# The mean of each residual norm is made by VectorE instead of GpSimd in a fused three-layer decoder kernel

## The chip, the cores and the metric

The kernel runs on one core of a Trainium2 chip. The metric is the device time of one execution in microseconds (us), smaller is better. All tensors are fp32; the matmuls run on operands split into a high and a low part (type fp32r).

## The reference, cut to what matters

Two blocks run one after the other on a residual `x` of 256 rows by 1024 columns. The first has two layers of mixer, cross-attention and SwiGLU, the second has one layer of three gated branches and a convolutional GLU. What matters here is the norm that opens each part:

```python
def rms_norm(x, gain):
    x32 = x.astype(jnp.float32)
    y = x32 * lax.rsqrt(jnp.mean(x32 * x32, axis=-1, keepdims=True) + RMS_EPS)
    return (y * gain.astype(jnp.float32)).astype(x.dtype)
...
    for layer in range(DEPTH):
        hn = rms_norm(x, g[0])                # mixer (norms 0 and 3 of the kernel)
...
        x = x + rms_norm(y, g[1])
        y = memory_cross_attention(rms_norm(x, g[2]), ...)   # norms 1 and 4
        x = x + rms_norm(y, g[3])
        y = swiglu_ffn(rms_norm(x, g[4]), ...)               # norms 2 and 5
        x = x + rms_norm(y, g[5])
...
    h = _rmsnorm(x, norm_mix_g[l])            # norm 6
    x = x + (merged @ w_out[l].astype(jnp.float32)).astype(x.dtype)
    h2 = _rmsnorm(x, norm_ffn_g[l])           # norm 7
```

## The kernel before, in words

The five engines run five programs that are written out by hand, in a fixed order on each, and meet at named semaphores. The residual lies in SBUF as two tiles of 128 rows by 1024 columns (`xr[:, t, :]`, t = 0 and 1), and `xn` holds the normed rows.

**Weights.** SyncE streams them in chunks of 1 MB, each cut into two pieces of 128x1024. ScalarE rounds a piece to its high part (`whi`, L1124) and VectorE subtracts to get the low part (`wlo`, L1663). TensorE multiplies with both. Both engines work up to four pieces ahead of TensorE (`past(name)` does all pieces up to four behind the chunk of that name). So between any two steps of the program VectorE and ScalarE have weight pieces to do, and their place in the order is fixed.

**A norm of the residual** (eight of them, `no` = 0 to 7) is a chain over four engines, for each of the two tiles:

1. ScalarE squares a tile with the row sums as accumulator (`squares`, L1142; norm 7 squares each half of a tile, L1624), semaphore `n_sq` (`half_sq`).
2. GpSimd makes the mean plus epsilon (L2291; L2427 in norm 7), waits on its own semaphore `pool_step`, and takes the power -0.5 (L2292; L2428), semaphore `n_r`. Both are on one column of 128 rows.
3. VectorE multiplies the tile with that column (`normed`, L1683), semaphore `n_x`.
4. TensorE turns the tile in eight 128x128 transposes (L472; L1093 in norm 7), ScalarE takes the high part with the gain (L1156; L1634) and VectorE the low part (`rest`, L1693; L2257), eight of each, semaphores `n_hi` and `n_lo`. The next matmuls (L388 to L390 of `fm`, L403 and L405 of `wide`, L418 and L420 of `wide_tile` in norm 7) wait for these.

Between the end of the block before and the matmuls that need the normed rows TensorE has filler work: products of the memory rows (`keys`, `values`, the `mk` and `mv` chunks), put before, between and behind the transposes. Norm 0, at the start, has none; norm 7 has the last pieces of the `mo` product. In norms 1 to 6 VectorE has two weight pieces (`past(...)`) between the last residual addition (`post_add`, L1715) and `normed`, and two more behind it, and often a copy out of PSUM (L1726), before the first `rest`.

Of the kernel before, what the change touches and what calls it, by code (L numbers as in the profile page):

```python
# [5 lines left out]
ALU = mybir.AluOpType  # L6
ACT = mybir.ActivationFunctionType
# [6 lines left out]
EPS = 1e-6  # L14
BIG = -1.0e30
D = 1024
# [9 lines left out]
h_A01m h_cp h_d h_e h_f h_m1 h_m2 h_n h_o h_q h_r h_sq h_z half_sq heads_T heads_a heads_d heads_n hg_act  # L26
hn_r hn_sq hn_ss ho_r ho_sq ho_ss lg_zero lo_first m2_act m2_dve mT_T mT_hi mT_lo m_T m_hi m_lo m_r m_sq m_x
mem0_in0 mem0_in1 mem1_in0 mem1_in1 mg mg0 ml_act ml_cols ml_dec ml_dve ml_hs ml_log ml_num ml_og ml_p ml_qk
ml_z mlv_act mlv_dve mo_add mt n_T n_hi n_lo n_r n_sq n_x out pa_m pa_r pa_sq pool_step resid row_in0 row_in1
row_in2 row_in3 row_in4 row_in5 sb_a sb_c sb_hi sb_k sb_ln sb_lo sb_q sb_t sb_v sb_w sb_z sbv_act sbv_dve  # L30
tm_first w_first w_hi w_lo w_raw0 w_raw1 w_raw2 w_used x_in0 x_in1 xe xm xo xo_hi xp xq xs xt xv xw ya_hi
ya_lo yb_hi yb_lo z_T z_hi z_lo
"""

SHARED = {
# [48 lines left out]
def build_program(nc, I, out):  # L84
    ctx = ExitStack()
    with ctx:
        def sb(name, shape, dt=F32):
            return ctx.enter_context(nc.sbuf_tensor(name, shape, dt))
# [6 lines left out]
        xr = sb("xr", [128, NT, D])  # L95
        xn = sb("xn", [128, NT, D])
# [13 lines left out]
        mhalf = sb("mhalf", [128, 8])  # L110
# [18 lines left out]
        def stats(n):  # L129
            return [(stat(n), stat(n), stat(n)) for _ in range(NT)]  # L130
# [140 lines left out]
        S = {}  # L271
# [14 lines left out]
        n_st = [stats(1) for _ in range(8)]  # L286
        half_sq = [(stat(1), stat(1)) for _ in range(NT)]
# [21 lines left out]
        xq = [reg(512 * i, 512).rearrange("p (k t) -> p k t", k=2) for i in range(3)]  # L309
# [800 lines left out]
        def scalar_program(act):  # L1110
# [25 lines left out]
            def squares(no):  # L1136
                for t in range(NT):
                    if no == 0:
                        act.wait_ge(S[f"x_in{t}"], 16)
                    else:  # L1140
                        act.wait_ge(S["resid"], 2 * no - 1 + t)
                    act.activation(xn[:, t, :], xr[:, t, :], ACT.Square, accum_out=n_st[no][t][0]).then_inc(S["n_sq"], 1)  # L1142

            def mem_squares(i):
                for t in range(NT):
# [160 lines left out]
            for t in range(NT):  # L1306
                act.wait_ge(S["ml_hs"], t + 1)
                for h in range(4):
                    if t or h:
                        act.wait_ge(S["h_sq"], 4 * t + h)  # L1310
                    act.activation(sq[:, 0:256], heads(xn[:, t, :], 4)[:, h, :], ACT.Square,
                                   accum_out=h_st[t][0][:, h:h + 1]).then_inc(S["h_sq"], 1)
# [8 lines left out]
            for k in range(8):  # L1321
                b, half = half_bank(k, (0, 1, 2, 3))
                act.wait_ge(S["z_T"], k + (1 if half else 3))
                if half:
                    act.wait_ge(S["z_lo"], k - 1)
                act.activation(XTh[:, k, :], ps[:, b, 256 * half:256 * half + 256], ACT.Copy,
                               scale=g[:, k:k + 1]).then_inc(S["z_hi"], 1)
# [322 lines left out]
        def vector_program(dve):  # L1650
# [28 lines left out]

            def normed(no, tiles=range(NT)):  # L1680
                for t in tiles:
                    dve.wait_ge(S["n_r"], 2 * no + t + 1)
                    dve.tensor_scalar(xn[:, t, :], xr[:, t, :], n_st[no][t][2], None, ALU.mult).then_inc(S["n_x"], 1)  # L1683

# [594 lines left out]
        def gpsimd_program(pool):  # L2279
            own = [0]  # L2280

            def step(i):
                own[0] += 1
                i.then_inc(S["pool_step"], 1)
                return own[0]

            def rstd(stat3, n, cnt, sem, need, done):

                ss, m, r = stat3
                pool.wait_ge(*at(sem, need))  # L2290
                pool.wait_ge(S["pool_step"], step(pool.tensor_scalar(m, ss, 1.0 / cnt, EPS, ALU.mult, ALU.add)))  # L2291
                pool.tensor_tensor(r, m, mhalf[:, 0:n], ALU.pow).then_inc(S[done], 1)  # L2292

            def norm(no):
                for t in range(NT):
                    rstd(n_st[no][t], 1, D, "n_sq", 2 * no + t + 1, "n_r")

            def mem_norm(i):
                for t in range(NT):
# [122 lines left out]
                        pool.wait_ge(S["mg"], 2 * n + t - 1)  # L2422
                    pool.tensor_tensor(dst, dst, bt[:, 512 * t:512 * t + 512], ALU.add).then_inc(S["mg"], 1)
            for t in range(NT):
                ss, m, r = n_st[7][t]
                pool.wait_ge(S["half_sq"], 2 * t + 2)
                pool.wait_ge(S["pool_step"], step(pool.tensor_scalar(m, half_sq[t][0], half_sq[t][1], EPS, ALU.add, ALU.add)))  # L2427
                pool.tensor_tensor(r, m, mhalf[:, 0:1], ALU.pow).then_inc(S["n_r"], 1)  # L2428


        def sync_program(sp):
# [67 lines left out]
```

## Time and profile before

| | |
|---|---|
| median of 3 runs | 1312.08 us (1310.54 to 1313.65) |
| the profiled execution: time | 1310.67 us |
| its span | 1308.9 us |
| TensorE busy | 1289.3 us, 99% of the span |
| VectorE busy | 882.5 us, 67% |
| ScalarE busy | 688.8 us, 53% |
| GpSimd busy | 111.0 us, 8% |
| chain that ended last, by engine | TensorE 90%, VectorE 5%, ScalarE 3%, GpSimd 1%, issue 1%, DMA 1% |

The span is the time from the first to the last instruction of the profiled execution; 1.8 us of its time lie outside it. TensorE sets the pace nearly everywhere; the shares of the other engines in the chain are the short places at which TensorE waited.

### The profile page before, as it was taken

The page shows a single profiled execution, that of the slowest core. Times are in us where ns is not written, and L with a number is a line of the kernel's source. Part 1 is how long each engine was busy: PE and PEld are TensorE (multiplying, and loading weights), DVE is VectorE, ACT ScalarE, POOL GpSimd, SP SyncE. Part 2 cuts the span into 40 slices and gives each one's busy share as a digit, 9 for nine tenths or more (in the row PEclk, how much of TensorE's full clock was granted, in tenths as well). Part 3 has the DMA queues.
Part 4 walks back from the last instruction along what each step waited for, and adds up shares of the span by engine and source line. Part 5 has one row for each costly group of instructions (what it writes and reads, how often), then busy time and mean ns, then how long its engine had stood idle before and what let it go on. Part 6 is the DMA issues. An engine that isn't in the chain of part 4 may idle for free.

```text
span 1308.9 us, 17685 instructions
## 1 busy us (share of the span) xinstructions
PE 1289.3 (99%) x7313; PEld 1109.8 (85%) x7313; DVE 882.5 (67%) x1035; ACT 688.8 (53%) x960; POOL 111.0 (8%) x176
## 2 busy tenths in 40 slices
PE   7999999999999999999999999999999999999999
PEld 6889897988888888788888888898877888888887
DVE  4566664776666676876576666767885566887775
ACT  4655554644444656564554444565555654654553
POOL 7200100100000100030100000101330003000000
PEclk9999999999999999999999999999999999999999
DMA  8753653555555543354356555563544435455552
GB/s 260 246 169 134 198 172 104 196 193 187 187 188 188 189 161 124 135 178 144 129 192 194 190 188 184 178 194 98 161 149 143 159 131 191 135 188 192 193 194 97
DMA packets 156113, 223.64 MB, mean 171 GB/s; under 512 B 6103, under 2 KB 107635, under 8 KB 156032
## 3 DMA queue, kind: packets, MB, share of 16 engines
q1 hardware_dynamic: 154240, 218.18, 50.7%
q0 software_dynamic: 1664, 4.27, 1.1%
q8 instruction: 58, 0.95, 0.3%
q14 instruction: 23, 0.19, 0.0%
q10 hardware_dynamic: 128, 0.05, 0.0%
HBM read 221.44 MB, written 1.05 MB: 170 GB/s over the span
## 4 chain that ended last, share of the span: by engine, by line
PE 90%; DVE 5%; ACT 3%; POOL 1%; issue 1%; DMA 1%; SPq 0%; ACTq 0%
PE ps L403 18%; PE ps L405 9%; PE ps L450 9%; PE ps L451 9%; PE ps L452 9%; PE ps L388 5%; PE ps L390 5%; PE ps L389 5%; PE ps L585 4%; PE ps L587 4%; PE ps L586 4%; DVE wlo L1663 2%; PE ps L897 1%; PE ps L472 1%; ACT whi L1124 1%; PE ps L520 1%
## 5 line engine op out<-in xcount | busy, mean ns | idle before, releaser
L1124 ACT ACTIVATE whi<-raw 128x1024 fp32r<-128x1024 f32 x412 | 425.9, 1052 | 347.1 <-PE ps L403 163.7
L1663 DVE TENSOR_TENSOR wlo<-raw,whi 128x1024 fp32r<-128x1024 f32 x411 | 492.9, 1229 | 169.8 <-ACT whi L1124 166.9
L403 PE MATMUL ps<-RR,whi 128*128 128x512 f32 x1040 | 359.1, 396 | 0.0
L405 PE MATMUL ps<-RR,wlo 128*128 128x256 f32 x1040 | 268.9, 279 | 0.1
L450 PE MATMUL ps<-whi,RR 128*128 128x512 f32 x592 | 238.3, 402 | 3.1 <-DVE ar L1726 1.6
L452 PE MATMUL ps<-whi,RR 128*128 128x512 f32 x592 | 231.0, 390 | 0.0
L451 PE MATMUL ps<-wlo,RR 128*128 128x512 f32 x592 | 231.0, 390 | 0.0
L403 PEld LDWEIGHTS ps<-RR,whi 128*128 128x128 f32 x1040 | 187.6, 188 | 35.9
L405 PEld LDWEIGHTS ps<-RR,wlo 128*128 128x128 f32 x1040 | 196.0, 188 | 12.1 <-DVE RR L1693 0.4
L388 PE MATMUL ps<-RR,whi 128*128 128x256 f32 x512 | 147.3, 288 | 2.9 <-DVE RR L1693 1.4
L390 PE MATMUL ps<-RR,wlo 128*128 128x256 f32 x512 | 144.8, 283 | 0.0
L389 PE MATMUL ps<-RR,whi 128*128 128x256 f32 x512 | 144.8, 283 | 0.0
L450 PEld LDWEIGHTS ps<-whi,RR 128*128 128x128 f32 x592 | 111.2, 188 | 30.3 <-issue 3.6
L452 PEld LDWEIGHTS ps<-whi,RR 128*128 128x128 f32 x592 | 111.1, 188 | 24.2
L451 PEld LDWEIGHTS ps<-wlo,RR 128*128 128x128 f32 x592 | 111.3, 188 | 21.2
L388 PEld LDWEIGHTS ps<-RR,whi 128*128 128x128 f32 x512 | 98.1, 192 | 6.3 <-DVE RR L1693 2.9
L585 PE MATMUL ps<-whi,RR 128*128 128x512 f32 x256 | 99.7, 389 | 0.0
L587 PE MATMUL ps<-whi,RR 128*128 128x512 f32 x256 | 99.6, 389 | 0.0
L586 PE MATMUL ps<-wlo,RR 128*128 128x512 f32 x256 | 99.6, 389 | 0.0
L389 PEld LDWEIGHTS ps<-RR,whi 128*128 128x128 f32 x512 | 98.1, 192 | 0.2
L390 PEld LDWEIGHTS ps<-RR,wlo 128*128 128x128 f32 x512 | 98.1, 192 | 0.0
L1764 DVE TENSOR_REDUCE ar<-ps 128x512 f32<-128x1024 f32 x33 | 40.4, 1225 | 74.0 <-PE ps L403 73.2
(337 smaller groups left out, 1279.2 us busy)
## 6 DMA issues: line engine op xcount, KB each, us to landing
raw<-in_ffn_w_gate_up SPq DMA_DIRECT2D x44, 1024.0 KB, 5.1
raw<-in_ffn_w_down SPq DMA_DIRECT2D x33, 1024.0 KB, 5.0
raw<-in_w_in SPq DMA_DIRECT2D x28, 1024.0 KB, 5.1
raw<-in_ffn_w_up SPq DMA_DIRECT2D x22, 1024.0 KB, 5.1
raw<-in_xa_w_kv SPq DMA_DIRECT2D x16, 1024.0 KB, 5.2
raw<-in_sb_w_qkv SPq DMA_DIRECT2D x12, 1024.0 KB, 5.1
raw<-in_ml_w_in SPq DMA_DIRECT2D x11, 1024.0 KB, 7.8
raw<-in_xa_w_q SPq DMA_DIRECT2D x8, 1024.0 KB, 5.3
```

The costliest lines, as they stand in the source:

```text
L388: pe.matmul(o, p.hi[:, k, :], X.h[:, k, :], start=k == 0, stop=False)
L389: pe.matmul(o, p.hi[:, k, :], X.l[:, k, :], start=False, stop=False)
L390: m = pe.matmul(o, p.lo[:, k, :], X.h[:, k, :], start=False, stop=k == 7)
L403: m = pe.matmul(two(ps[:, bank, :]), p.hi[:, k, :], XT2[:, k, :, :], start=k == 0, stop=k == 7)
L405: pe.matmul(ps[:, bank, 0:256], p.lo[:, k, :], X.h[:, k, :], start=False, stop=False)
L450: pe.matmul(o, X.h[:, g, r], p.hi[:, k, :], start=g == 0, stop=False)
L451: pe.matmul(o, X.h[:, g, r], p.lo[:, k, :], start=False, stop=False)
L452: m = pe.matmul(o, X.l[:, g, r], p.hi[:, k, :], start=False, stop=g == K - 1)
L585: pe.matmul(o, h[:, i, r], p.hi[:, 0, c], start=j == 0 and i == 0, stop=False)
L586: pe.matmul(o, h[:, i, r], p.lo[:, 0, c], start=False, stop=False)
L1124: act.activation(p.hi, p.raw, ACT.Copy).then_inc(S["w_hi"], 1)
L1663: dve.tensor_tensor(p.lo, p.raw, p.hi.bitcast(F32), ALU.subtract).then_inc(S["w_lo"], 2 if p.n == 2 else 1)
```

## The change

ScalarE squares `x / 32` instead of `x` (a scale of the same activation, 1024 ** -0.5), so that its row sums are already the means. VectorE adds epsilon in `normed`, ahead of each tile's multiplication: for norms 0 to 6 it waits for ScalarE's sum, for norm 7 it adds the two halves' sums and epsilon. GpSimd waits for that (new semaphore `n_m`) and takes the power alone. The other uses of GpSimd's `rstd` (`post_norm`, `mem_norm`, the head norms) stay as they are.

```diff
-                    act.activation(xn[:, t, :], xr[:, t, :], ACT.Square, accum_out=n_st[no][t][0]).then_inc(S["n_sq"], 1)
+                    act.activation(xn[:, t, :], xr[:, t, :], ACT.Square, scale=D ** -0.5,
+                                   accum_out=n_st[no][t][0]).then_inc(S["n_sq"], 1)
...
             def normed(no, tiles=range(NT)):
                 for t in tiles:
+                    ss, m, r = n_st[no][t]
+                    if no < 7:
+                        dve.wait_ge(S["n_sq"], 2 * no + t + 1)
+                        dve.tensor_scalar(m, ss, EPS, None, ALU.add).then_inc(S["n_m"], 1)
+                    else:
+                        dve.wait_ge(S["half_sq"], 2 * t + 2)
+                        dve.tensor_scalar(m, half_sq[t][0], half_sq[t][1], EPS, ALU.add, ALU.add).then_inc(S["n_m"], 1)
                     dve.wait_ge(S["n_r"], 2 * no + t + 1)
                     dve.tensor_scalar(xn[:, t, :], xr[:, t, :], n_st[no][t][2], None, ALU.mult).then_inc(S["n_x"], 1)
...
+            def root(no, t):
+
+                ss, m, r = n_st[no][t]
+                pool.wait_ge(S["n_m"], 2 * no + t + 1)
+                pool.tensor_tensor(r, m, mhalf[:, 0:1], ALU.pow).then_inc(S["n_r"], 1)
+
             def norm(no):
                 for t in range(NT):
-                    rstd(n_st[no][t], 1, D, "n_sq", 2 * no + t + 1, "n_r")
+                    root(no, t)
...
             for t in range(NT):
-                ss, m, r = n_st[7][t]
-                pool.wait_ge(S["half_sq"], 2 * t + 2)
-                pool.wait_ge(S["pool_step"], step(pool.tensor_scalar(m, half_sq[t][0], half_sq[t][1], EPS, ALU.add, ALU.add)))
-                pool.tensor_tensor(r, m, mhalf[:, 0:1], ALU.pow).then_inc(S["n_r"], 1)
+                root(7, t)
```

First, VectorE's order at norm 4, from the last residual addition of the block before (L1715, L1723 in the changed file) to the first low parts of the turned rows. Before:

```order
L1715 SCALAR_TENSOR_TENSOR xr<-xn,st,xr 128x1024 [waits pa_r,pa_m]
L1663 TENSOR_TENSOR wlo<-raw,whi 128x1024 [waits w_hi] x2
L1683 TENSOR_SCALAR xn<-xr,st 128x1024 [waits n_r] x2
L1678 COPY gcol<-ps 128x88 [waits gains_T]
L1663 TENSOR_TENSOR wlo<-raw,whi 128x1024 [waits w_hi] x2
L1693 SCALAR_TENSOR_TENSOR RR<-ps,gcol,RR 128x256 [waits n_hi] x8
```

And with the change (every line number is a few higher, so L1691 is the multiplication that was L1683):

```order
L1723 SCALAR_TENSOR_TENSOR xr<-xn,st,xr 128x1024 [waits pa_r,pa_m]
L1664 TENSOR_TENSOR wlo<-raw,whi 128x1024 [waits w_hi] x2
L1686 TENSOR_SCALAR st<-st 128x1 [waits n_sq]
L1691 TENSOR_SCALAR xn<-xr,st 128x1024 [waits n_r]
L1686 TENSOR_SCALAR st<-st 128x1 [waits n_sq]
L1691 TENSOR_SCALAR xn<-xr,st 128x1024 [waits n_r]
L1679 COPY gcol<-ps 128x88 [waits gains_T]
L1664 TENSOR_TENSOR wlo<-raw,whi 128x1024 [waits w_hi] x2
L1701 SCALAR_TENSOR_TENSOR RR<-ps,gcol,RR 128x256 [waits n_hi] x8
```

The additions stand in VectorE's queue behind the two weight pieces, and the second tile's addition behind the first tile's multiplication. Norms 1, 2, 3, 5 and 6 have the same five rows around `xn<-xr,st`.

Second, the same engine at norm 7, from the additions of the two half products into the residual (L2250; L2258 in the changed file) to the second tile's multiplication. Before:

```order
L2250 TENSOR_TENSOR xr<-xr,ps 128x512 [waits tm_first] x2
L1683 TENSOR_SCALAR xn<-xr,st 128x1024 [waits n_r]
L2250 TENSOR_TENSOR xr<-xr,ps 128x512 [waits w_used]
L1663 TENSOR_TENSOR wlo<-raw,whi 128x1024 [waits w_hi] x2
L2257 SCALAR_TENSOR_TENSOR RR<-ps,gcol,RR 128x128 [waits n_hi] x4
```

And with the change:

```order
L2258 TENSOR_TENSOR xr<-xr,ps 128x512 [waits tm_first] x2
L1689 TENSOR_SCALAR st<-st 128x1 [waits half_sq]
L1691 TENSOR_SCALAR xn<-xr,st 128x1024 [waits n_r]
L2258 TENSOR_TENSOR xr<-xr,ps 128x512 [waits w_used]
L1664 TENSOR_TENSOR wlo<-raw,whi 128x1024 [waits w_hi] x2
```

Here nothing stands between the half products' additions and the new instruction.

Third, GpSimd's order around norm 4, between its DMA of the second memory and the norm of that memory (`m_sq`). Before:

```order
L2390 DMA ar<-in_mem 128x1024
L2291 TENSOR_SCALAR st<-st 128x1 [waits n_sq]
L2292 TENSOR_TENSOR st<-st,mhalf 128x1 [waits pool_step]
L2291 TENSOR_SCALAR st<-st 128x1 [waits n_sq]
L2292 TENSOR_TENSOR st<-st,mhalf 128x1 [waits pool_step]
L2291 TENSOR_SCALAR st<-st 128x1 [waits m_sq]
L2292 TENSOR_TENSOR st<-st,mhalf 128x1 [waits pool_step]
```

And with the change (L2306 is the power in `root`):

```order
L2404 DMA ar<-in_mem 128x1024
L2306 TENSOR_TENSOR st<-st,mhalf 128x1 [waits n_m] x2
L2299 TENSOR_SCALAR st<-st 128x1 [waits m_sq]
L2300 TENSOR_TENSOR st<-st,mhalf 128x1 [waits pool_step]
L2299 TENSOR_SCALAR st<-st 128x1 [waits m_sq]
```

GpSimd now waits for VectorE where it waited for ScalarE, and has one instruction per tile and no wait on itself.

## Rows read from the trace of the kernel before

**Rows 1.** The page: busy time (share of the span) and instructions

```profile
PE 1289.3 (99%) x7313; PEld 1109.8 (85%) x7313; DVE 882.5 (67%) x1035; ACT 688.8 (53%) x960; POOL 111.0 (8%) x176
PEclk9999999999999999999999999999999999999999
```

**Rows 2.** Who TensorE waited for: us in total, times, longest

```profile
PE ps L472 <- DVE xn L1683: 2.7, 1, 2.7
...
PE ps L388 <- DVE RR L1693: 1.4, 3, 0.5
```

**Rows 3.** The chain that ended last, around norm 6: start, us, what

```profile
844.89 1.41 POOL st L2292
846.39 0.76 POOL st L2291
847.23 0.56 POOL st L2292
847.81 0.75 DVE xn L1683
...
852.97 0.39 PE ps L388
```

**Rows 4.** Timeline at norm 6: start, us, instruction, [idle before <-releaser]

```profile
843.54 2.35 DVE L1663 TENSOR_TENSOR wlo<-raw,whi 128x1024 fp32r<-128x1024 f32 x2
...
846.34 0.75 DVE L1683 TENSOR_SCALAR xn<-xr,st 128x1024 f32<-128x1024 f32 x1 [0.45 <-POOL st L2292]
```

**Rows 5.** One line of VectorE: a TENSOR_SCALAR on one column

```profile
L2138 DVE TENSOR_SCALAR st<-gcol x1: 145/145/145, 962.1 to 962.1; 128x1 f32<-128x1 f32 x1
```

**Rows 6.** Timeline: a small result handed from VectorE to GpSimd

```profile
945.64 0.69 DVE L2112 TENSOR_REDUCE st<-ar 128x4 f32<-128x512 f32 x1 [0.84 <-ACT ar L1521]
946.42 0.20 POOL L2291 TENSOR_SCALAR st<-st 128x4 f32<-128x4 f32 x1 [7.08 <-DVE st L2112]
```

**Rows 7.** Chain around norm 5

```profile
658.81 0.39 PE ps L405
```

**Rows 8.** Timeline at norm 3

```profile
435.46 2.35 DVE L1663 TENSOR_TENSOR wlo<-raw,whi 128x1024 fp32r<-128x1024 f32 x2
...
440.00 0.76 DVE L1683 TENSOR_SCALAR xn<-xr,st 128x1024 f32<-128x1024 f32 x1 [0.72 <-POOL st L2292]
...
445.16 0.39 PE L388 MATMUL ps<-RR,whi 128*128 128x256 f32 x1 [0.50 <-DVE RR L1693]
```

**Rows 9.** Timeline at norm 4

```profile
571.14 2.36 DVE L1663 TENSOR_TENSOR wlo<-raw,whi 128x1024 fp32r<-128x1024 f32 x2
571.36 1.43 POOL L2292 TENSOR_TENSOR st<-st,mhalf 128x1 f32<-128x1 f32 x1
574.61 0.75 DVE L1683 TENSOR_SCALAR xn<-xr,st 128x1024 f32<-128x1024 f32 x1 [0.44 <-POOL st L2292]
...
578.78 1.66 DVE L1693 SCALAR_TENSOR_TENSOR RR<-ps,gcol,RR 128x256 fp32r<-128x256 f32 x4 [0.21 <-ACT RR L1156]
579.83 0.28 PE L388 MATMUL ps<-RR,whi 128*128 128x256 f32 x1
```

**Rows 10.** Timeline at norm 7, first tile

```profile
1111.52 0.19 ACT L1624 ACTIVATION_READ_ACCUMULATOR xn<-xr 128x1 f32 x1
1112.20 0.57 POOL L2428 TENSOR_TENSOR st<-st,mhalf 128x1 f32<-128x1 f32 x1
1112.81 0.75 DVE L1683 TENSOR_SCALAR xn<-xr,st 128x1024 f32<-128x1024 f32 x1 [1.86 <-POOL st L2428]
1116.84 0.36 PE L418 MATMUL ps<-RR,whi 128*128 128x256 f32 x1 [0.27 <-DVE RR L2257]
```

**Rows 11.** Chain in the first 20 us

```profile
2.16 7.47 DMA raw<-in_ml_w_in
```

**Rows 12.** Timeline behind norms 1 and 2, VectorE

```profile
157.92 4.98 DVE L1663 TENSOR_TENSOR wlo<-raw,whi 128x1024 fp32r<-128x1024 f32 x4
...
247.99 1.23 DVE L1663 TENSOR_TENSOR wlo<-raw,whi 128x1024 fp32r<-128x1024 f32 x1 [0.46 <-ACT whi L1124]
```

More of the change, by code:

```diff
@@ L28 @@
 mem0_in0 mem0_in1 mem1_in0 mem1_in1 mg mg0 ml_act ml_cols ml_dec ml_dve ml_hs ml_log ml_num ml_og ml_p ml_qk
[L29 to L32, printed above, removed]
+ml_z mlv_act mlv_dve mo_add mt n_T n_hi n_lo n_m n_r n_sq n_x out pa_m pa_r pa_sq pool_step resid row_in0
+row_in1 row_in2 row_in3 row_in4 row_in5 sb_a sb_c sb_hi sb_k sb_ln sb_lo sb_q sb_t sb_v sb_w sb_z sbv_act
+sbv_dve tm_first w_first w_hi w_lo w_raw0 w_raw1 w_raw2 w_used x_in0 x_in1 xe xm xo xo_hi xp xq xs xt xv xw
+ya_hi ya_lo yb_hi yb_lo z_T z_hi z_lo
 """
```

## Prediction

> **What bounds the kernel now.** I read the page first: TensorE is busy 99% of the span at the full granted clock, VectorE 67%, GpSimd 8% [rows 1]. A change to GpSimd and VectorE can therefore only move time where TensorE waits for the result. The waits of TensorE come next: in all, it waited 2.7 us once for `xn` (norm 0, at the start) and 1.4 us in three places for the low parts of the turned rows [rows 2]. The chain that ended last then says which of these lead back through a norm's GpSimd steps. At norm 6 it does: power, mean, power on GpSimd, VectorE's multiplication, and 5 us later the matmul that had waited [rows 3]. The chain runs the same way to TensorE's wait at 658.81 behind norm 5 [rows 7], to that at 445.16 behind norm 3 [rows 8], and through norm 7's first tile [rows 10]. At norm 0 it goes through the DMA of the first weights instead [rows 11]; at norms 1, 2 and 4 it stays on TensorE.
>
> So the change is priced norm by norm, and the number wanted for each is when VectorE's *second* multiplication ends, since the weight pieces, the copy and the low parts behind it run in one unbroken row.
>
> **The new path, once.** Prices: the addition on one column 0.145 us, from VectorE's own one-column TENSOR_SCALAR [rows 5]; VectorE to GpSimd 0.09 us (945.64 + 0.69 = 946.33 to 946.42) [rows 6]; the power undisturbed 0.56 us [rows 3] to 0.57 us [rows 10], of which I take 0.55 in norms 0 to 6, since the chain's pieces reach to the next one's start; GpSimd to VectorE 0.04 us (1112.77 to 1112.81) [rows 10]. VectorE starts an instruction for which nothing is awaited about 0.08 us before the profile's end of the one before it. From the end of what VectorE did before, the path "add, hand over, power, hand back" is then -0.08 + 0.145 + 0.09 + 0.55 + 0.04 = 0.745 us.
>
> **Norm 6, and norm 5 like it.** Before, GpSimd works while VectorE does its two weight pieces (843.54 to 845.89). The mean is done and the power issued at 844.89, and it ended at 846.30, only 0.41 us after the pieces, though alone it takes 0.55 [rows 3, 4]. VectorE multiplied at 846.34. With the change the addition stands behind the pieces: multiplication at 845.89 + 0.745 = 846.63, +0.29. Second tile: before, GpSimd's mean ran under the multiplication (846.34 to 847.09) and ended at 847.15, 0.06 us behind it; power at 847.23, multiplication at 847.81, that is 0.72 us after the first one's end [rows 3]. Now it is 0.745, so +0.30 in all after rounding.
> The stretched GpSimd rows (0.76 instead of 0.19, ending with a VectorE instruction) are the wait for the shared port. The Trainium skill, "SBUF — State Buffer", section "Who interferes with whom", says that the loser of that port fully blocks for the other's whole instruction, and its section on the wrong bandwidth intuition gives "DVE-end + ~115 ns" before it goes on. By that, the power would have ended at 845.89 + 0.115 + 0.55 = 846.56, the change would cost only 0.07 + 0.03 us at norms 5 and 6, and the sum below would be about 0.4 us smaller; the row has 846.30, so part of the power had been done behind the lock, and I take the row.
> At norm 6 TensorE's matmul at 852.97 follows VectorE directly [rows 3]: **+0.30**. Norm 5 has the same order on all engines, and TensorE waited at 658.81 in its chain [rows 7]: **+0.30**.
>
> **Norm 3.** ScalarE's sum came late, so that little of GpSimd's work lay under the weight pieces, which end at 437.81; the second multiplication began at 440.00 [rows 8]. With the change: first multiplication at 438.555, second 0.75 + 0.745 later at 440.05. TensorE at 445.16 follows: **+0.05**.
>
> **Norm 4.** Here ScalarE's sums came early and the first power had ended (571.36 + 1.43 = 572.79) before the weight pieces did (573.50): the first multiplication waited for nothing, and the second began at 574.61 [rows 9]. With the change: 573.50 + 0.745 = 574.245, ends 574.995; the second at 574.995 + 0.745 = 575.74, that is 1.13 late. What is late next: TensorE's transposes of the second tile, by less than that, and then the low parts, which all move by 1.13. One of them takes (1.66 + 3 x 0.08) / 4 = 0.475 us; the third ends at 578.78 + 0.475 + 1.13 = 580.385, and TensorE, which began to use it at 579.83 without a wait [rows 9], begins at 580.45. **+0.62**, in which the transposes' delay is contained. Behind that VectorE idles between weight pieces as it does behind norm 2 [rows 12], and makes its delay good.
>
> **Norm 7.** ScalarE's sum is there at 1111.71, VectorE is idle. Before: multiplication at 1112.81 [rows 10]. Now: 0.04 (nearest row, GpSimd to VectorE; ScalarE to GpSimd would be 0.11) + 0.16 (my estimate for the addition with a column as its second operand, a little over the 0.145) + 0.09 + 0.57 + 0.04 = 1112.61. TensorE's wait at 1116.84 is in this chain. **-0.20**. The second tile gains as much, but TensorE reaches its transposes after `xn` is there, so it adds nothing.
>
> **Norms 0, 1, 2.** At norm 0 the multiplications come some 0.15 us earlier; the chain there is a DMA until 9.63 us and ScalarE's rounding behind it [rows 11], which hide it (uncovered it would be worth -0.15). At norms 1 and 2 VectorE is 0.30 late as at norm 6. Behind norm 1 the four weight pieces take 4.98 us where two take 2.35, so they hold 0.3 us of waits for ScalarE that absorb it; behind norm 2 the low parts end 0.46 us before VectorE's next weight piece is ready [rows 12], and TensorE waits in neither stretch. **0** each; without this cover +0.6 together.
> ScalarE's scale adds no instruction. GpSimd loses sixteen small instructions: it is idle anyway.
>
> **Sum.** 0.30 + 0.30 + 0.05 + 0.62 - 0.20 = +1.07 us. The profiled execution would go from 1310.67 to 1311.7 us. That one lies 1.4 us under the median of the runs, 1312.08, so against the median I give **1313.1 us**, +0.08%. Changes under 0.2% (2.6 us; the three runs before spread over 3.1 us) can't be told from none.
>
> **Bounds.** The addition could cost less on the path only if VectorE began it earlier, which its order excludes; if the first power before the change had hidden nothing at norms 5 and 6 (it then could not end before 845.89 + 0.55 = 846.44, 0.14 later than it did) and norm 4's delay meets 0.3 us of slack that I don't see, the sum is 1.07 - 0.28 - 0.3 = +0.5. If the additions take 0.25 us and nothing covers norms 1 and 2, it is 1.07 + 0.6 + 8 x 0.1 = +2.5.
>
> **Rivals.**
> *The chain shortens (faster).* Counting only GpSimd's steps, the chain at norm 6 holds a mean of 0.76 us [rows 3]; if each tile of norms 3, 5 and 6 lost that and got 0.15 instead, 6 x 0.6 = 3.6 us would go, 1308.5. Against it: most of each 0.76 is VectorE's own work, under which the mean ran; taking it away does not bring VectorE's next result sooner. It decides if GpSimd's power starts while VectorE still works, which the order forbids. 3 in 100.
> *Nothing arrives (same).* TensorE's waits at norms 4 to 6 are met by slack the trace doesn't show: 1312.1. 15 in 100.
> *The granted clock falls (slower).* Norm 4 adds pauses of 0.6 us in all to a stretch in which TensorE ran without one. Were the clock to be granted at 1.2 GHz instead of 2.4 behind it, each us of TensorE's work costs another; it decides when more than 1.5 us of work fall in it, and 4 us of it give 1317. Against it: the page has 9 or more tenths in all forty slices, though TensorE waited 2.7 us at once at the start [rows 1, 2]. 4 in 100. The Trainium skill, "TensorE: Matmul & The Clock Gate", section "What's actually happening", says that idleness brings the throttle back; the pauses here are far shorter than the one at the start, behind which the rows show none.
> *The late VectorE work piles up (slower, by the same path).* All eight norms uncovered and the dearer addition: the +2.5 above, 1314.6, just under what can be told. 8 in 100.
> The forecast has the remaining 70.
>
> **Chances.** Faster by over 0.2%: 0.03, the first rival. Slower by over 0.2%: the clock, a part of the last rival, and the median's own scatter on top of +1.07, together 0.09. Same: 0.88. The range reaches from the case in which nothing arrives (1312.1) less 0.9 us of scatter to the +2.5 (1314.6) and 0.4 us of it: 1311.2 to 1315.0.
>
> **What would show it.** Around norm 4 (from 570 us) the second `xn` multiplication starts about 2.2 us after the second weight piece's end instead of 1.1, and the first L388 after the transposes shows a wait of 0.3 to 0.6 us for the low parts. At norms 5 and 6 each multiplication starts 0.75 us after the end of VectorE's work before it. The power is 0.55 us at all sixteen places, never 1.43. At norm 7 the gap from ScalarE's sum to the multiplication is 0.9 instead of 1.1 us. The prediction is wrong if a power is still stretched, if the addition takes over 0.25 us, or if TensorE's row of busy time shows new waits outside the norms.

## The result, and the profile after

| | before | changed |
|---|---|---|
| median | 1310.74 us (22 runs, 1310.08 to 1313.65) | 1313.18 us (22 runs, 1311.63 to 1315.70) |
| ratio | | 1.0017, 95% interval 1.0011 to 1.0023 |
| the profiled execution: time, span | 1310.67, 1308.9 us | 1312.99, 1311.2 us |

The medians are 2.44 us apart, 0.19%, just within what I took as no difference. The interval excludes 1.0: the change costs a little. (The ratios here are the recorded ones; they are not quotients of the two medians, which would be 1.0019 in this table.) The times of either kernel lie in groups. The lowest seven runs of the changed one are 1311.63 to 1311.71 us; the lowest fourteen of the kernel before are 1310.08 to 1310.8. These groups are about 1.1 us apart, the rest of the 2.44 lies in how many runs fall in higher groups. Both parts are followed below.

The page of the changed kernel, busy time and the chain by engine:

```profile
PE 1291.6 (99%) x7313; PEld 1111.2 (85%) x7313; DVE 883.8 (67%) x1051; ACT 688.8 (53%) x960; POOL 96.3 (7%) x160
PE 90%; DVE 6%; ACT 2%; issue 1%; DMA 1%; POOL 0%; SPq 0%; ACTq 0%
```

Sixteen instructions and 14.7 us left GpSimd, sixteen and 1.3 us came to VectorE, and of the chain GpSimd's 1% is gone, VectorE has 6% instead of 5 and ScalarE 2% instead of 3. Beside [rows 1] this reads like a relief; it is none. The timeline at norm 6, VectorE and then GpSimd, shows why (start, us, instruction, idle before and who ended it):

```profile
845.82 2.35 DVE L1664 TENSOR_TENSOR wlo<-raw,whi 128x1024 fp32r<-128x1024 f32 x2
848.09 0.14 DVE L1686 TENSOR_SCALAR st<-st 128x1 f32<-128x1 f32 x1
848.90 0.75 DVE L1691 TENSOR_SCALAR xn<-xr,st 128x1024 f32<-128x1024 f32 x1 [0.66 <-POOL st L2306]
849.57 0.14 DVE L1686 TENSOR_SCALAR st<-st 128x1 f32<-128x1 f32 x1
850.38 0.75 DVE L1691 TENSOR_SCALAR xn<-xr,st 128x1024 f32<-128x1024 f32 x1 [0.66 <-POOL st L2306]
...
848.32 0.55 POOL L2306 TENSOR_TENSOR st<-st,mhalf 128x1 f32<-128x1 f32 x1 [4.08 <-DVE st L1686]
849.79 0.55 POOL L2306 TENSOR_TENSOR st<-st,mhalf 128x1 f32<-128x1 f32 x1 [0.93 <-DVE st L1686]
```

The pieces end at 848.17 and the multiplication starts at 848.90, 0.73 behind them; in [rows 4] it was 0.45. GpSimd, which used to work under the pieces, sits idle 4.08 us until VectorE has added. For the second tile the gap from multiplication to multiplication is 0.73 (849.65 to 850.38) against 0.72 in [rows 3].

At norm 4 the loss is largest. VectorE, then TensorE:

```profile
572.35 2.35 DVE L1664 TENSOR_TENSOR wlo<-raw,whi 128x1024 fp32r<-128x1024 f32 x2
574.62 0.15 DVE L1686 TENSOR_SCALAR st<-st 128x1 f32<-128x1 f32 x1
575.45 0.75 DVE L1691 TENSOR_SCALAR xn<-xr,st 128x1024 f32<-128x1024 f32 x1 [0.68 <-POOL st L2306]
576.11 0.15 DVE L1686 TENSOR_SCALAR st<-st 128x1 f32<-128x1 f32 x1
576.93 0.75 DVE L1691 TENSOR_SCALAR xn<-xr,st 128x1024 f32<-128x1024 f32 x1 [0.67 <-POOL st L2306]
...
581.10 1.66 DVE L1701 SCALAR_TENSOR_TENSOR RR<-ps,gcol,RR 128x256 fp32r<-128x256 f32 x4 [0.21 <-ACT RR L1157]
...
577.74 1.09 PE L472 MATMUL ps<-ident,xn 128*128 128x128 f32 x8 [0.22 <-DVE xn L1691]
...
581.64 0.39 PE L388 MATMUL ps<-RR,whi 128*128 128x256 f32 x1
581.87 0.28 PE L389 MATMUL ps<-RR,whi 128*128 128x256 f32 x1
```

The second multiplication starts 2.23 us behind the pieces, as forecast (1.11 in [rows 9]). TensorE now waits before the second tile's transposes. At the first L388 the row names no wait, but it started 8.02 us behind the wait at 573.62 that both kernels have, 7.41 before (579.83 - 572.42): 0.61 late. Of these, 0.41 were there behind the transposes already; the other 0.20 came at this L388, which starts at 581.64, right behind the third low part (the first of the row at 581.10, some 0.48 us long). And its successor follows after 0.23 instead of 0.11 us.

At norm 7 the addition has two columns and takes 0.22 us; the multiplication starts 0.92 behind ScalarE's sum (1114.05 + 0.18 = 1114.23), where it was 1.10 [rows 10]. The rows of ScalarE, VectorE and GpSimd:

```profile
1114.05 0.18 ACT L1625 ACTIVATION_READ_ACCUMULATOR xn<-xr 128x1 f32 x1
...
1114.27 0.22 DVE L1689 TENSOR_SCALAR st<-st 128x1 f32<-128x1 f32 x1 [0.79 <-ACT xn L1625]
1115.15 0.75 DVE L1691 TENSOR_SCALAR xn<-xr,st 128x1024 f32<-128x1024 f32 x1 [0.67 <-POOL st L2306]
...
1114.56 0.56 POOL L2306 TENSOR_TENSOR st<-st,mhalf 128x1 f32<-128x1 f32 x1 [16.03 <-DVE st L1689]
```

**Where the two profiled executions part.** I compared the same event in both. Norm 3's first L388 is at 445.16 before and 446.34 after, yet only 0.01 of these 1.18 us arises at norm 3 (the post-norm work ahead of it is at 432.78 and 433.95). The rest is older than norm 1. TensorE's rows in the first microseconds of matmuls of the changed kernel,

```profile
12.33 0.41 PE L389 MATMUL ps<-RR,whi 128*128 128x256 f32 x1
12.54 0.41 PE L390 MATMUL ps<-RR,wlo 128*128 128x256 f32 x1
...
15.74 0.41 PE L390 MATMUL ps<-RR,wlo 128*128 128x256 f32 x1
15.96 0.31 PE L388 MATMUL ps<-RR,whi 128*128 128x256 f32 x1
```

and of the kernel before,

```profile
12.29 0.28 PE L389 MATMUL ps<-RR,whi 128*128 128x256 f32 x1
12.41 0.28 PE L390 MATMUL ps<-RR,wlo 128*128 128x256 f32 x1
```

follow each other by 0.21 us in one and 0.12 in the other, for 4 us. What comes before is alike in both: the sixteen transposes of norm 0 take 3.68 us, where those of norm 4 take 1.91 (here of the kernel before):

```profile
7.92 3.68 PE L472 MATMUL ps<-ident,xn 128*128 128x128 f32 x16 [2.74 <-DVE xn L1683]
...
575.32 1.91 PE L472 MATMUL ps<-ident,xn 128*128 128x128 f32 x16
```

So TensorE starts at about half its pace in either execution, behind the wait of 2.7 us, and keeps it until about 12 us in one and 16 us in the other. The profile's windows print a granted clock of 1.00 there, but this is no measurement: the trace's record of the granted clock has its first entry, at full clock, only at 11.7 us (before) and at 16.0 us (changed), and the windows count what lies ahead of it as full. In each trace with the slow step it ends where that record begins: at 13.4 us in e4, 13.9 in e8, 14.0 in e10, 16.7 in e1. The slow first microseconds are thus read as TensorE's 1.2 GHz level. When it ends differs between executions of the same instructions (16.0 us here, 16.7 in e1; 13.9 and 14.0 in e8 and e10; 11.6 and 11.0 in e6 and e7, which have the changed norm 0 too), so it is a matter of the execution. By the shift of the same matmul against the kernel before it is worth 1.2 us here and 1.6 in e1, 0 to 0.5 in the other traces. It accounts for a group of runs 1.3 us above the lowest (1312.92 to 1313.16 at a mean granted clock of 1.0, the profiled one among them).

### The profile page after: what moved, and what is told of

It is laid out like the page before. It is cut to its first block, busy times and chain, and to the rows that moved or that the text cites. A ratio compares the mean times of both kernels' runs of the same rounds, so it can differ in the third digit from the quotient of the medians.

```text
span 1311.2 us, 17685 instructions
## 1 busy us (share of the span) xinstructions
PE 1291.6 (99%) x7313; PEld 1111.2 (85%) x7313; DVE 883.8 (67%) x1051; ACT 688.8 (53%) x960; POOL 96.3 (7%) x160
## 4 chain that ended last, share of the span: by engine, by line
PE 90%; DVE 6%; ACT 2%; issue 1%; DMA 1%; POOL 0%; SPq 0%; ACTq 0%
PE ps L403 18%; PE ps L405 9%; PE ps L450 9%; PE ps L452 8%; PE ps L451 8%; PE ps L388 5%; PE ps L390 5%; PE ps L389 5%; PE ps L585 4%; PE ps L587 4%; PE ps L586 4%; DVE wlo L1664 2%; PE ps L897 1%; PE ps L472 1%; PE ps L520 1%; PE ps L499 1%
## 5 line engine op out<-in xcount | busy, mean ns | idle before, releaser
L405 PE MATMUL ps<-RR,wlo 128*128 128x256 f32 x1040 | 269.0, 279 | 0.1
L405 PEld LDWEIGHTS ps<-RR,wlo 128*128 128x128 f32 x1040 | 196.0, 188 | 12.1 <-DVE RR L1701 0.4
L388 PE MATMUL ps<-RR,whi 128*128 128x256 f32 x512 | 148.1, 289 | 3.0 <-DVE RR L1701 1.5
L389 PE MATMUL ps<-RR,whi 128*128 128x256 f32 x512 | 145.6, 284 | 0.0
L388 PEld LDWEIGHTS ps<-RR,whi 128*128 128x128 f32 x512 | 99.0, 193 | 6.7 <-DVE RR L1701 3.3
L389 PEld LDWEIGHTS ps<-RR,whi 128*128 128x128 f32 x512 | 99.0, 193 | 0.2
```

The costliest lines, as they stand in the source:

```text
L388: pe.matmul(o, p.hi[:, k, :], X.h[:, k, :], start=k == 0, stop=False)
L389: pe.matmul(o, p.hi[:, k, :], X.l[:, k, :], start=False, stop=False)
L405: pe.matmul(ps[:, bank, 0:256], p.lo[:, k, :], X.h[:, k, :], start=False, stop=False)
```

## The experiments

Each was timed in eleven runs beside the kernel before. "Least" is the range of its lowest group of times. The results also hold each run's mean granted clock of TensorE over the span: 1.0, 0.999 or 0.997 (and once 0.949). Where lowest groups of two kernels are compared below, it is by their medians.

**e1, the changed kernel again.** No edit.

> The changed kernel once more, unchanged. Theory A (fixed path cost of about +1.1 us in every run, from norms 3 to 7, and on top of it a granted clock that differs from run to run): the fastest runs are 1311.6 to 1311.7 us, against 1310.1 to 1310.6 for the kernel before, and the runs fall into groups at +1.3 and about +4 us above the fastest; the +4 group has a mean granted clock of 0.997. Rival B (the median's +2.2 us is all path cost): no run is under 1312.5 us. The profile tells which place of the program ran at the lower granted clock, if this run is of such a group.

Median 1313.85 us, ratio 1.0021 (1.0012 to 1.0030). Nine of eleven runs have a clock of 0.997. The windows around norm 7, of this execution (us, busy time of each engine, granted clock, DMA):

```profile
1115.00:1120.00 5.00, 4.91 (x28) 3.90 (x27) 4.17 (x7) 3.46 (x8) 0.55 (x1) 1.00 0.00 0
1120.00:1125.00 5.00, 4.48 (x23) 3.65 (x22) 3.35 (x9) 3.94 (x9) 0.56 (x1) 0.76 0.64 211
1125.00:1130.00 5.00, 5.00 (x26) 4.82 (x26) 1.61 (x6) 1.81 (x7) 0.00 (x0) 0.56 0.00 0
```

and one row ahead of the fall and one in it, of TensorE:

```profile
1121.48 0.33 PE L420 MATMUL ps<-RR,wlo 128*128 128x128 f32 x1 [0.36 <-DVE RR L2265]
...
1125.27 0.52 PE L418 MATMUL ps<-RR,whi 128*128 128x256 f32 x1
```

The granted clock falls to its 1.2 GHz level behind norm 7's first tile and is back before 1130 us. What TensorE did before is L418 and L420, products of 256 and 128 columns, with a wait of 0.36 us in them. The same stretch of the profiled changed kernel shows 1.00 throughout, with the same waits. So there is a second group effect: such runs are about 2.2 us over the lowest group (1313.8 against 1311.65), or 3.9 where the slow first microseconds come on top (1315.5 to 1315.7). Such runs are in the kernel before as well, 4 of these 33. The runs at 0.999 have a shorter fall at the same place. Of the traces below, e3, e4, e5 and e8 (0.999) show 3.4 us at the lower level, e6 and e7 (0.997) 6.8 as e1; all seven falls begin between 1119.4 and 1122.6 us. By the shift of the same matmul across it, the short fall costs 1.5 to 1.6 us and the long one 2.2.

**e2, the change at norm 4 alone; e3, at norms 0 and 7 alone.** Later e6 and e7 were made in the same way, by a list of the norms that take the new path:

```diff
+ON = (4,)           # e2; e3: (0, 7); e6: (0, 1, 2, 3, 4, 5, 6); e7: (0, 1, 2, 3, 5, 6, 7)
...
-                    act.activation(xn[:, t, :], xr[:, t, :], ACT.Square, scale=D ** -0.5,
-                                   accum_out=n_st[no][t][0]).then_inc(S["n_sq"], 1)
+                    act.activation(xn[:, t, :], xr[:, t, :], ACT.Square,
+                                   scale=D ** -0.5 if no in ON else 1.0, accum_out=n_st[no][t][0]).then_inc(S["n_sq"], 1)
...
                 ss, m, r = n_st[no][t]
-                pool.wait_ge(S["n_m"], 2 * no + t + 1)
+                if no not in ON:
+                    if no < 7:
+                        rstd(n_st[no][t], 1, D, "n_sq", 2 * no + t + 1, "n_r")
+                        return
...
```

> VectorE makes the mean at norm 4 alone; all other norms are as before. By the term of the sum the span's path grows by 0.6 to 0.75 us: the second multiplication of norm 4 starts 2.2 us behind the end of the weight pieces, and the floor of the runs lies 0.6 to 0.75 us over the floor of the kernel before (1310.1 to 1310.6). Theory C (it is norm 4's delay that brings the runs with a mean clock of 0.997): such runs, about 4 us longer, are here too. Its rival D (they come from the start of the program, or from nothing in the change): they are here no more often than with the kernel before.

Median 1312.88 us, ratio 1.0007 (0.9998 to 1.0015). Least 1310.98 to 1311.30 us, where the kernel before has most of its lowest group at 1310.5 to 1310.7: +0.6 to +0.7, the term of norm 4.

> VectorE makes the means at norms 0 and 7 alone. By the terms: norm 7 gives -0.20 us, norm 0 nothing (hidden under the first weights' DMA), so the floor is 0.2 us under that of the kernel before and the first tile's multiplication of norm 7 starts 0.9 us behind ScalarE's sum instead of 1.1. If norm 0's earlier transposes matter for the granted clock, the runs at +4 us and a mean clock of 0.997 are here; if norms 1 to 6 bring them, they are not.

Median 1311.84 us, ratio 1.0 (0.9991 to 1.0009). Least 1310.22 to 1310.41, some 0.2 below before's. Five of its eleven runs lie at 1311.6 to 1312.0 with a clock of 1.0, which lifts its median. I take them for runs with slow first microseconds, but no trace shows one: the profiled run (1311.96, clock 0.999) has the 0.12 us step from the start and owes its 1.6 us to a short fall at 1120.4 us. No run is at 0.997.

**e4, both tiles' additions ahead of the first multiplication**, norms 0 to 6:

```diff
             def normed(no, tiles=range(NT)):
+                if no < 7:
+                    for t in tiles:
+                        ss, m, r = n_st[no][t]
+                        dve.wait_ge(S["n_sq"], 2 * no + t + 1)
+                        dve.tensor_scalar(m, ss, EPS, None, ALU.add).then_inc(S["n_m"], 1)
                 for t in tiles:
                     ss, m, r = n_st[no][t]
-                    if no < 7:
-                        dve.wait_ge(S["n_sq"], 2 * no + t + 1)
-                        dve.tensor_scalar(m, ss, EPS, None, ALU.add).then_inc(S["n_m"], 1)
-                    else:
+                    if no == 7:
...
```

> As the changed kernel, but in norms 0 to 6 VectorE makes the means of both tiles before it multiplies the first tile, so that GpSimd's second power can run under that multiplication. If the price of the second tile is the serial path (0.745 us from the first multiplication's end), it falls to 0.3 to 0.5 us, as at norm 4 before the change (0.45): the second multiplication comes 0.15 us later from the extra addition and 0.3 us sooner from the overlap, and the floor is 0.1 to 0.2 us lower at each of norms 3, 4, 5 and 6, some 0.5 us in all under the changed kernel's 1311.65. If the shared port makes the power wait for the whole multiplication, nothing is gained and the floor is 0.5 us higher than the changed kernel's.

Median 1309.71 us (1309.62 to 1311.86), ratio 0.9992 (0.9983 to 1.0001). Least 1309.62 to 1309.81: 2.0 below the changed kernel, where I had expected 0.5, and 0.9 below the kernel before. The timeline at norm 6:

```profile
845.48 0.21 DVE L1686 TENSOR_SCALAR st<-st 128x1 f32<-128x1 f32 x2
846.29 1.58 DVE L1693 TENSOR_SCALAR xn<-xr,st 128x1024 f32<-128x1024 f32 x2 [0.60 <-POOL st L2308]
...
845.71 1.38 POOL L2308 TENSOR_TENSOR st<-st,mhalf 128x1 f32<-128x1 f32 x2 [4.08 <-DVE st L1686]
846.22 0.86 POOL L2308 TENSOR_TENSOR st<-st,mhalf 128x1 f32<-128x1 f32 x1
```

(The last row is the second of the two powers by itself.)

and at norm 3, where ScalarE's second sum comes late:

```profile
438.67 0.15 DVE L1686 TENSOR_SCALAR st<-st 128x1 f32<-128x1 f32 x1 [0.53 <-ACT xn L1142]
438.81 0.75 DVE L1693 TENSOR_SCALAR xn<-xr,st 128x1024 f32<-128x1024 f32 x1
440.00 0.75 DVE L1693 TENSOR_SCALAR xn<-xr,st 128x1024 f32<-128x1024 f32 x1 [0.44 <-POOL st L2308]
...
438.22 1.75 POOL L2308 TENSOR_TENSOR st<-st,mhalf 128x1 f32<-128x1 f32 x2 [4.08 <-DVE st L1686]
```

At norm 6 the second power stands ready behind the first and starts just ahead of VectorE's multiplication. It takes 0.86 us instead of 0.55, but VectorE's multiplication over it takes its usual 0.75. It ends at 847.09, 0.05 behind it (846.29 + 0.75 = 847.04), and the second multiplication follows at once: two rows of VectorE in 1.58 us. At norm 3 the second power becomes ready only when the multiplication is already under way; it ends at 439.97, 0.41 behind it, and VectorE waits 0.44 us. The same 0.44 and 0.45 stand in [rows 4, 9]. So the wait for the port depends on who is first: a power that is first ends 0.05 us behind the multiplication over it, one that is second 0.4 us behind it.

How near this can run shows at norm 3 of the kernel before, where GpSimd's mean of the second tile and the first tile's multiplication start together. Norm 3 is untouched in e2, e3, e5 and e9; in the first three it looks as in the kernel before (first two rows), in e9 as in the last two:

```profile
438.53 0.75 DVE L1683 TENSOR_SCALAR xn<-xr,st 128x1024 f32<-128x1024 f32 x1 [0.72 <-POOL st L2292]
438.58 0.75 POOL L2291 TENSOR_SCALAR st<-st 128x1 f32<-128x1 f32 x1
...
438.45 0.79 DVE L1685 TENSOR_SCALAR xn<-xr,st 128x1024 f32<-128x1024 f32 x1 [0.72 <-POOL st L2294]
438.50 0.19 POOL L2293 TENSOR_SCALAR st<-st 128x1 f32<-128x1 f32 x1
```

Both means start 0.05 us behind the multiplication. One is held for its whole length; the other takes 0.19 us and VectorE's row is 0.04 longer. TensorE's first L388 of norm 3 then comes 0.26 us earlier in e9. So an execution of the kernel before can be 0.26 us better at norm 3 than the profiled one, and the price of the change there is 0.01 or 0.27 us by which of the two it is compared with.

**e5, the kernel before with the path made longer**, to see whether the runs with a fallen clock come with the edit or with the delay:

```diff
                     dve.wait_ge(S["n_r"], 2 * no + t + 1)
+                    if t == 1 and no in (5, 6):
+                        dve.wait_ge(S["dve_step"], step(dve.tensor_scalar(xn[:, t, 0:768], xr[:, t, 0:768], n_st[no][t][2], None, ALU.mult)))
                     dve.tensor_scalar(xn[:, t, :], xr[:, t, :], n_st[no][t][2], None, ALU.mult).then_inc(S["n_x"], 1)
```

> The kernel before with nothing of the change in it; at norms 5 and 6 VectorE does 768 columns of the second tile's multiplication once more ahead of the whole one (the same values are written twice). That is about 0.56 + 0.08 us on the path at each, +1.3 us in all, which is the sum that the changed kernel paid. Its least times should therefore lie near 1311.7 us, as the changed kernel's do, under every theory. They part in the other runs, those in which the granted clock falls near norm 7 (some 3 or 7 us at the 1.2 GHz level in the trace). Theory A: the share of such runs follows from how late norm 7 comes, whatever made it late: more than half of this kernel's runs show a mean clock under 1.0 (before: 12 of 33; changed: 9 of 11), median 1312.5 to 1313.8. Rival: the share follows from the change's own work at norm 7 (additions on VectorE, the shorter gap): a third of the runs as before, median 1311.7 to 1312.2.

Median 1314.11 us, before 1312.13 (33 runs), ratio 1.0017 (1.0008 to 1.0026), the very ratio of the change. Least 1312.00 to 1312.08, 1.3 over the lowest group of the kernel before; norm 6's first L388 is at 854.27, 1.30 later than in [rows 3]. Eight of eleven runs have a clock under 1.0, six of them 0.997, against 17 and 5 of 33 of the kernel before. Nothing of the change is in this kernel.

**e6, the change without norm 7.**

> The change at norms 0 to 6, norm 7 as before (its mean on GpSimd). The sum of my terms gives +1.27 over before: least times at 1311.8 us, 0.2 above those of the changed kernel. Theory A (the fallen clock depends on how late norm 7 comes): most runs under 1.0 in clock, median 1313 to 1314. Rival (it depends on the edit at norm 7): a third of them, median near 1312.

Median 1313.66 us, ratio 1.0015 (1.0006 to 1.0024). Least 1312.04 to 1312.15. In its trace the first matmul behind norm 6's wait (L389 in its file) is 1.26 later than in [rows 3] and has no slow first microseconds in it: this is the cleanest measurement of norms 1 to 6, for which my terms give 1.27. Five of eleven runs are at 0.997. So the addition at norm 7 is not what lets the clock fall.

**e7, the change without norm 4.**

> The change at all norms but norm 4, which has its mean on GpSimd as before. Norm 4 cost 0.73 us in the trace, so the least times should be 1311.65 - 0.73 = 1310.9 us; if norm 4's loss is given back behind it they stay at 1311.65. The share of runs with a fallen clock lies between that of before and that of the changed kernel by theory A, since norm 7 comes 0.7 us later than before instead of 1.4; median 1311 to 1313.

Median 1312.87 us, ratio 1.0007 (0.9998 to 1.0016); a single run in the lowest group, 1311.22. Its norm 6 is 0.63 later than in [rows 3], 0.63 less than e6's: norm 4 is half of the whole, and its loss is not given back. Nine of eleven runs are under 1.0, two of them at 0.997.

**e8, e4 with the additions one weight piece earlier** at norms 4, 5 and 6 (norm 5 shown):

```diff
-            past("xo1_3")
+            lo_to(end("xo1_3") + NSP - 1)
+            adds(5)
+            past("xo1_3")
             normed(5)
```

> Both tiles' additions together at norms 0 to 6, and at norms 4, 5 and 6 one weight piece earlier, so that GpSimd's two powers meet the second piece of VectorE (1.17 us) instead of an idle VectorE. Theory: a power that is issued while VectorE works is served in part behind it (at norm 6 of the kernel before it ended 0.41 us after the pieces, not 0.55), so the first multiplication starts 0.1 to 0.4 us after the pieces instead of 0.75, and the second directly behind it: 0.3 to 0.6 us less per norm than with both additions first, least times 1308.2 to 1308.8 us. Rival 1, VectorE's instruction holds off the whole power: multiplication 0.6 us after the pieces, 0.1 less per norm, 1309.4. Rival 2, TensorE does not wait at these norms any more (it had no wait at norms 4 and 6 with both additions first): nothing arrives, 1309.7.

Median 1309.42 us (1309.20 to 1311.61), before 1312.13, ratio 0.9984 (0.9976 to 0.9993); least 1309.20 to 1309.47. Its norm 6:

```profile
844.87 0.15 DVE L1685 TENSOR_SCALAR st<-st 128x1 f32<-128x1 f32 x1 [0.23 <-ACT xn L1142]
844.94 1.22 DVE L1664 TENSOR_TENSOR wlo<-raw,whi 128x1024 fp32r<-128x1024 f32 x1
846.07 1.57 DVE L1696 TENSOR_SCALAR xn<-xr,st 128x1024 f32<-128x1024 f32 x2
...
844.72 2.13 POOL L2311 TENSOR_TENSOR st<-st,mhalf 128x1 f32<-128x1 f32 x2 [2.95 <-DVE st L1685]
```

The first multiplication follows the second piece without any gap, which is more than the theory gave (0.1 to 0.4 us behind it): here too the first power was first. Yet the least time fell by 0.4, not by 0.9 to 1.4. TensorE is why: it had little wait left in e4. My expectation said none at norms 4 and 6, which was wrong. At norm 6 the first L388 of e4 (first row) starts 0.42 us behind the matmul before it and is one of those that follow a wait (0.39 us long), in e8 (second row) 0.23:

```profile
852.27 0.39 PE L388 MATMUL ps<-RR,whi 128*128 128x256 f32 x1
...
852.23 0.29 PE L388 MATMUL ps<-RR,whi 128*128 128x256 f32 x1
```

That is 0.3 us with the slower successor; at norm 4 e4 had 0.1 left. At norm 5 the kernel before has small waits, one at each L405 as a low part comes, of which e4 keeps two and e8 none: 0.33 us for L405 in the kernel before, 0.28 in e8 (first row):

```profile
658.41 0.28 PE L405 MATMUL ps<-RR,wlo 128*128 128x256 f32 x1
```

```profile
658.18 0.32 PE L405 MATMUL ps<-RR,wlo 128*128 128x256 f32 x1
```

From behind norm 3 to norm 7 TensorE gains 1.1 us over the kernel before in e8's trace and 0.7 in e4's, which is the 0.4. So rival 2 of this run is nearly right: with the last waits gone, a still earlier multiplication brings nothing.

**e9, e5 with the longer path for both tiles** (`if no in (5, 6):` instead of `if t == 1 and no in (5, 6):`).

> The kernel before; at norms 5 and 6 VectorE does 768 columns of each tile's multiplication once more ahead of the whole one, both tiles now (the same values are written twice), so twice the delay of e5. Path: least times at 1310.5 + 2 x 1.4 = 1313.3 us. Theory A in its plain form (the later norm 7 comes, the more runs show the long fall of the granted clock, 0.997): 7 or more of 11 runs at 0.997, median over 1315.5. If only the place in time counts and not how late it is, the share may as well go back to that of before (under a sixth at 0.997), median near 1314; that would leave the size of the delay as no explanation.

Median 1314.04 us, before 1310.73 (21 runs), ratio 1.0018 (1.0009 to 1.0027). Least 1312.43 to 1312.97, not the 1313.3 expected. From norm 3's L388 to norm 6's it takes 409.89 us (444.83 to 854.72), 0.74 more than in e5 (445.12 to 854.27) instead of 1.3. VectorE's added row of the second tile at norm 6 waits 0.44 us for the power, where in e5 it waits 0.71: the first tile's longer work covers GpSimd's mean, which I had overlooked, and the power ends 0.4 behind it. One run of eleven at 0.997, though norm 7 comes later than in any other kernel, the first microseconds left out. Theory A in its plain form falls with it.

**e10, e8 once more.**

> The kernel of e8 once more, to see whether it beats both kernels on another day: least times 1309.2 us, at most 1 run in 4 at a granted clock of 0.997, median 1309.3 to 1311.1, faster than before by 0.7 to 1.6 us in the least times. If e8's median rested on lucky runs, the ratio's interval takes in 1.0.

Median 1310.89 us (1309.08 to 1311.63), before 1310.73, ratio 0.9991 (0.9982 to 1.0). Least 1309.08 to 1309.41 against 1310.27 to 1310.98: 1.3 us faster in its lowest group, as e8 (1.4). But six runs of eleven are under 1.0 here, four at 0.997, where e8 had four and one. The share differs between two sets of runs of one kernel as much as between kernels.

| kernel | runs at a mean clock of 0.997 | norm 7 comes, against before |
|---|---|---|
| e8, e10 | 5 of 22 | 1.4 us earlier |
| e4 | 2 of 11 | 1.0 earlier |
| e3, before | 9 of 98 | within 0.2 |
| e2, e7 | 6 of 22 | 0.6 to 0.7 later |
| changed (with e1), e5, e6 | 29 of 55 | 1.2 to 1.4 later |
| e9 | 1 of 11 | 1.9 later |

The last column is from the traces: the shift of TensorE's matmul at 1115 us of the kernel before, less the shift that is there at 100 us, which leaves out the slow first microseconds. One run of the kernel before has a mean clock of 0.949 at 1312.39 us, no longer than its neighbours at 0.999; it is not counted.

## Why the prediction was right, and what was luck in it

**The path.** By its own steps: norm 3 +0.05 predicted, +0.01 measured (+0.27 against an execution as e9's); norm 4 +0.62 and +0.73; norm 5 +0.30 and +0.34; norm 6 +0.30 and +0.29; norm 7 -0.20 and -0.20; norms 0 to 2 nothing, and nothing found (the shift of +1.20 ahead of norm 1 is +1.17 ahead of norm 3). Together +1.07 and +1.17 us, e6 says 1.26 for the first four terms, and the lowest groups of runs 1.1. The new path of 0.745 us was 0.73 at norm 6 and 0.75 at norm 4. Every power takes 0.55 or 0.56 us now, none is stretched.

**Norm 4 was mis-sized by 0.11.** The start of L388 came 0.61 late, as computed, and behind the low part that I had named. The sign that I had given for it came only in part: not a wait of 0.3 to 0.6 us at L388, but 0.41 at the transposes and 0.20 there. I had left out that the first matmul behind a wait is followed after 0.23 us instead of 0.11; [rows 8] had shown such a row at norm 3 with 0.39 instead of 0.28. A norm at which TensorE did not wait and now does pays this once more; norms 3, 5 and 6 had it paid already, or wait in small pieces.

**What the sum explains and what it doesn't.** My 1313.1 was worked from the median of three runs, 1312.08; 22 runs put the kernel before at 1310.74. The changed one came out at 1313.18. The number is therefore met by +1.1 of the path and 1.3 of a base that was too high. The medians differ by 2.44, twice my sum. The remainder is in the two group effects of the executions: the slow first microseconds (+1.2 to +1.6) and the fall of the granted clock at norm 7 (+1.5 and +2.2). The prediction had neither as a term, only as scatter; that the measured median met its 1313.1 is luck.

**The clock rival.** I gave it 4 in 100, placed it behind norm 4, and argued that a 2.7 us pause at the start left no mark on the clock row. The granted clock does fall, at norm 7: e1 shows it for the changed kernel, e5 for the one before with a delay in it, and in one set 5 of 33 runs of the kernel before have the mean clock of the long fall. The argument looked at one execution, and the fall wasn't in it. Its premise doesn't hold either: behind the pause at the start TensorE did run at the lower level, until 11.7 us in that very execution, and the row of [rows 1] can't show it because the record of the clock begins only there. Its price was too high as well: I let 4 us of TensorE's work cost 4 us. The windows of e1 show 2.4 and 4.4 us at the lower level (twice 0.24 and twice 0.44 of 5 us), 6.8 in all and so some 3.4 us of work, and such runs are 2.2 us longer: I take a part of it to lie under TensorE's waits for VectorE, which no run tested. That more runs of the changed kernel have it (18 of 33 against 9 of 87 at 0.997) is measured. That it comes from the delay and not from the edit is supported by e5, which has the delay alone (6 of 11, beside 5 of 33), and e6, which has no edit at norm 7 (5 of 11). That a later norm 7 as such does it is contradicted by e9 (1 of 11). With eleven runs of a kernel these shares are rough: e8 and e10, the same kernel, have 1 and 4. Which property of the execution decides, and so whether the change makes the fall likelier at all, stays open.

**The other rivals.** The shortened chain (1308.5) did not come, for the reason given: the mean on GpSimd had lain under VectorE's work. "Nothing arrives" is excluded by e5: a pure delay of 1.3 us on this path arrives whole, 1.30 at norm 6 and 1.3 in the lowest groups. "The late work piles up" is excluded at norms 1 and 2 by the unchanged shift between them.

**The rule on the port.** The Trainium skill, "SBUF — State Buffer", section "Who interferes with whom", has the loser fully blocked for the other's whole instruction. For a power second to a multiplication the runs agree in kind: it ends 0.41 us behind it (e4, norm 3). For one that is first they do not: the multiplication that started 0.07 us behind it took its usual 0.75 us, and it was the power that took 0.86 and ended 0.05 behind (e4, norm 6). By the same page's figure of some 115 ns before the loser goes on (section "A bandwidth-pool intuition that's wrong (but worth ruling out)", where it is told of a DMA's descriptors behind a copy), it is my estimate that a power of 0.55 us would end 0.67 behind; 0.41 is measured at norms 3 and 6, and the measurement decides. That let me price norms 5 and 6 at +0.30 each, where the rule would have given 0.07 + 0.03; +0.34 and +0.29 came.

**What I did not see.** The better order was in my own reading. What cost time was not which engine adds, but that both adding and the power of the second tile waited behind VectorE's first multiplication. With both additions first (e4) the same change gains 0.9 us over the kernel before in the lowest group, and 1.3 to 1.4 with them one weight piece earlier (e8, e10). Of their medians only e8's is faster than before beyond doubt.

## What to carry to other kernels

A small step taken from an idle engine and put on a busy one, in order behind its long work, costs its handover again, however short the chain by engine then looks; price the order in which the results come, tile by tile. Where GpSimd and VectorE share work, let GpSimd's short instruction become ready before VectorE's long one starts: first, it ended 0.05 us behind it, second, 0.4. And for differences near 0.2%, compare the lowest groups and the granted clock of many runs before the medians: here half of the difference of the medians was not in the path's added waits, and three runs of before had a median 1.3 us off. Before a granted clock of 1.00 is taken for full pace at a kernel's start, compare the steps of its first matmuls with later ones.

## What the runs showed of the hardware that I had not expected

- TensorE starts this kernel at its lower level: norm 0's sixteen transposes take 3.68 us (3.54 in e3), norm 4's 1.91. The first full-clock entry of the clock's record comes between 11.0 and 16.7 us, at another time in each execution, and until then products of 256 columns step at 0.21 us instead of 0.12. It is worth up to 1.6 us.
- The granted clock falls to the 1.2 GHz level at norm 7 (0.76 and 0.56 in two windows of 5 us of e1) though TensorE was busy 4.91 of the 5 us before, with a wait of 0.36 us. In seven of twelve traces it falls there, for 3.4 or 6.8 us.
- A mean on GpSimd that starts 0.05 us behind VectorE's multiplication took 0.75 us in four traces and 0.19 in one (norm 3 of the kernels that leave it as before).
- A one-column TENSOR_SCALAR with a column as its second operand takes 0.22 us, with a constant 0.14 to 0.15.
